# A chunked delta-rule scan rebuilt from 64x64 quarter products, in a four-layer kernel on one core

## The reference

```python
def step(state, inp):                      # state: 64x64 for each head
    r_t, w_t, k_t, v_t, kk_t, b_t = inp
    sa = jnp.einsum('bhij,bhj->bhi', state, kk_t)
    state = (state * w_t[:, :, None, :] - sa[..., None] * b_t[:, :, None, :]
             + v_t[..., None] * k_t[:, :, None, :])
    y_t = jnp.einsum('bhij,bhj->bhi', state, r_t)
    return state, y_t
_, y = lax.scan(step, s0, (seq_first(rh), seq_first(wh), seq_first(kh),
                           seq_first(vh), seq_first(kk), seq_first(bh)))
...
y = group_norm(y) * ln_w + ln_b + bonus    # then * silu(gate), @ w_out
```

## Time and profile before

| | us |
|---|---|
| median of 3 runs | 1167.2 (1166.43 to 1167.28) |
| the profiled execution | 1165.14 |
| its span, first to last instruction | 1162.9 |
| the scan: first product of chunk 0 to the first product of the embedding behind it | 249.8 to 327.3 |
| PE busy over the span | 1130.6 (97%) |
| DVE, ACT, POOL busy | 735.5, 609.0, 465.5 |

### The profile page before, as it was taken

How to read it: one execution, slowest core, us unless ns; L and a number is a source line. 1 busy time by engine, 2 the same in 40 slices (tenths; PEclk the granted TensorE clock), 3 DMA queues, 4 the chain that set the end, 5 groups by cost and what they waited for, 6 DMA issues and landing times.

```text
span 1162.9 us, 19410 instructions
## 1 busy us (share of the span) xinstructions
PE 1130.6 (97%) x7558; PEld 885.5 (76%) x7558; DVE 735.5 (63%) x1166; ACT 609.0 (52%) x1026; POOL 465.5 (40%) x375
## 2 busy tenths in 40 slices
PE   7999999989999999999999999999999999999998
PEld 5756767878867887777777778878888888867776
DVE  6769996966675466666666484473593234567773
ACT  6867445536754466566655554462211344566563
POOL 2331024557733543333332344444454445532240
PEclk9999999999999999999999999999999999999999
DMA  9912446343183633212222123533333333322111
GB/s 285 273 55 73 89 112 217 109 138 80 46 296 97 193 94 90 74 56 73 69 59 73 55 91 93 164 89 88 97 102 91 101 98 91 91 73 67 62 55 73
DMA packets 194684, 123.02 MB, mean 106 GB/s; under 512 B 27877, under 2 KB 181030, under 8 KB 194214
## 3 DMA queue, kind: packets, MB, share of 16 engines
q1 hardware_dynamic: 191990, 119.27, 34.9%
q10 hardware_dynamic: 2608, 2.56, 0.7%
HBM read 105.03 MB, written 16.78 MB: 105 GB/s over the span
## 4 chain that ended last, share of the span: by engine, by line
PE 39%; issue 24%; POOL 12%; DVE 10%; DMA 1%; ACT 1%; POOLq 0%; ACTq 0%; DVEq 0%; SPq 0%
POOL b_w_lo L672 12%; PE banks L760 9%; PE banks L762 9%; PE banks L761 9%; DVE b_problems L2388 2%; DVE b_sum_squares L2386 2%; PE banks L1413 1%; PE banks L1441 1%; DVE b_suffix L2871 1%; PE banks L1020 1%; DMA b_problems<-d_a 1%; PE banks L767 1%; DVE b_a_lo L2217 1%; PE banks L1423 1%; DVE b_h_t L2213 1%
## 5 line engine op out<-in xcount | busy, mean ns | idle before, releaser
L672 POOL TENSOR_TENSOR b_w_lo<-b_w_raw,b_w_hi 128x512 fp32r<-128x512 f32 x296 | 399.5, 1371 | 637.8 <-ACT b_w_hi L1518 637.7
L760 PE MATMUL banks<-b_a_lo,b_w_hi 128*128 128x512 f32 x1232 | 496.6, 403 | 7.8 <-POOL b_w_lo L672 3.4
L762 PE MATMUL banks<-b_a_hi,b_w_lo 128*128 128x512 f32 x1232 | 482.1, 391 | 0.0
L761 PE MATMUL banks<-b_a_hi,b_w_hi 128*128 128x512 f32 x1232 | 481.1, 390 | 0.0
L1518 ACT ACTIVATE b_w_hi<-b_w_raw 128x1024 fp32r<-128x1024 f32 x156 | 164.9, 1057 | 255.1 <-PE banks L762 249.0
L760 PEld LDWEIGHTS banks<-b_a_lo,b_w_hi 128*128 128x128 f32 x1232 | 231.9, 188 | 72.0 <-issue 16.7
L762 PEld LDWEIGHTS banks<-b_a_hi,b_w_lo 128*128 128x128 f32 x1232 | 231.7, 188 | 50.2
L761 PEld LDWEIGHTS banks<-b_a_hi,b_w_hi 128*128 128x128 f32 x1232 | 232.2, 188 | 44.2 <-issue 0.5
L1956 ACT ACTIVATE b_exps<-banks,b_stats 128x128 f32<-128x128 f32 (+3 forms) x64 | 33.2, 524 | 58.3 <-DVE b_stats L2655 58.3
L2511 DVE SCALAR_TENSOR_TENSOR b_a_lo<-b_x_t,b_params,b_a_hi 128x512 fp32r<-128x512 f32 x32 | 34.3, 1085 | 23.5 <-ACT b_a_hi L1858 23.5
L2653 DVE TENSOR_TENSOR banks<-banks,b_consts 128x256 f32<-128x256 f32 x32 | 13.8, 433 | 46.3 <-PE banks L1269 45.1
(11 more groups left out here) (358 smaller groups left out, 1568.2 us busy)
## 6 DMA issues: line engine op xcount, KB each, us to landing
b_w_raw<-rw_w_in SPq DMA_DIRECT2D x32, 512.0 KB, 4.3
b_w_raw<-da_w_in SPq DMA_DIRECT2D x32, 512.0 KB, 4.0
b_w_raw<-w_in_a SPq DMA_DIRECT2D x32, 512.0 KB, 4.0
b_w_raw<-pe_w_gate SPq DMA_DIRECT2D x16, 512.0 KB, 4.2
d_ple<-b_ple_out SPq DMA_DIRECT2D x16, 256.0 KB, 4.5
b_w_raw<-rw_w_out SPq DMA_DIRECT2D x8, 512.0 KB, 4.1
b_ple_in<-d_ple SPq DMA_DIRECT2D x2, 2048.0 KB, 10.4
b_w_raw<-da_w_out SPq DMA_DIRECT2D x8, 512.0 KB, 3.9
```

What stands on the lines that cost most here:

```text
L672: m = pool.tensor_tensor(WLO[:, u % 2, ks], WRAW[:, u, ks], WHI[:, u % 2, ks].bitcast(F32), ALU.subtract)
L760: pe.matmul(dst, hi, a_lo[:, k_act, :], start=first, stop=False)
L761: pe.matmul(dst, hi, a_hi[:, k_act, :], start=False, stop=False)
L762: return pe.matmul(dst, lo, a_hi[:, k_act, :], start=False, stop=last)
```

## The change

- The stacked operands are taken apart. `w_of` becomes `w_values` (masked products with v) and `w_state` (K with the state); `s_of` becomes two calls of `s_part`, one for v and one for u; `y_chunk` becomes four calls of `y_part`. All sums are made in PSUM as before.
- Each product now has 64x64 operands. On which side (partitions 0 to 63 or 64 to 127) a head's operand lies alternates by tile (`side_w`, `side_u`), so that neighbours in the order use different quarters.
- `products` no longer makes the NB-K product: KH is multiplied with K and R (128 columns), NB with R alone (64 columns).
- `rows_of` turns by products with a 64x64 identity, 32 of them a chunk, in place of 8 transposes of 128x128.
- POOL's copies (`place_kt`, `place_v`) are gone. `scale_state` is one operation of 128x512 in place of two of 64x512.
- Copies out of PSUM span 128 partitions: keeping w, u, rows and masked products takes fewer and wider operations on ACT and DVE. ACT makes the table of decays that fits the new placing once (`order_decays`).
- PE's order in a chunk is new, and the parts that need v alone (w, s and y) are put where u and the state are waited for. The first embedding product is split and put into the last chunk.

Cut to its core (the placing of buffers, SP's store of the NB-K products and the checks of other waits left out):

```diff
+def side_w(h, j):
+    return h ^ j % 2
+def side_u(h, j):
+    return h ^ j % 2 ^ j // 2 % 2
+STRAIGHT, CROSSED = ([j for j in range(NT) if side_u(0, j) == n] for n in range(2))
...
-        def place_kt(c):
-            for h, hp in enumerate((low, up)):
-                pool.tensor_copy(XA[hp, :, h, :], KRX[hp, 0, :, chunk(c)]).then_inc(sem("kt_placed"), 1)
-        def place_v(dst, n):
-            for h, hp in enumerate((up, low)):
-                pool.tensor_copy(dst(hp, h), VS[hp, n // 2, :, :]).then_inc(sem("v_placed"), 1)
...
-        def rows_of(c, g):
-            turn_four(NKB, [NKP[:, 4 * g + m].rearrange("p n t -> p (n t)") for m in range(4)]).then_inc(sem("rows_mm"), 1)
+        def rows_of(c, kinds):
+            for kind in kinds:
+                for j in range(NT):
+                    for h, hp in enumerate(halves):
+                        m = pe.matmul(RB_[h][halves[side_u(h, j)], four(256 * kind, j // 2)], NKP[hp, j, kind, :], IDENT[hp, hp], ...)
...
-        def w_of(c):
-            for j in range(NT):
-                for h, hp in enumerate((low, up)):
-                    m = pe.matmul(WB[h][hp, tile_cols(j)], XA[:, j, h, :], SVX[c % 2][:, j, h, :], ...)
+        def w_values(c, tiles):
+            for j in tiles:
+                for h in range(2):
+                    at = halves[side_u(h, j)]
+                    m = pe.matmul(WB[h][halves[side_w(h, j)], four(0, j // 2)], XA[at, j // 4, h, j // 2 % 2, :], VS[at, c, j, :], ...)
+        def w_state(c):
+            pe.wait_ge(sem("state_done"), c)
             for j in range(NT):
+                for h, hp in enumerate(halves):
+                    m = pe.matmul(WB[h][halves[side_w(h, j)], four(0, j // 2)], KRX[hp, 0, j, chunk(c)],
+                                  ST[hp, c % 2, side_u(h, j), j // 2, :], ...)
...
-        def s_of(c):
-                    m = pe.matmul(SB[hp, tile_cols(j)], NKR[:, c % 2, j, h, :], UV[:, j, h, :], ...)
+        def s_part(c, kind):
+                    m = pe.matmul(RB_[b][hp, four(0, j // 2)], NKR[halves[b], h, kind, j // 2, :], VS[halves[b], c, j, :] if kind else u_at(h, j), ...)
-        def y_chunk(c):
-                    m = pe.matmul(y_at(h, j), UV[:, j, h, :], XR[:, c % 2, j, h, :], start=False, ...)
+        def y_part(c, tiles, kind):
+                    m = pe.matmul(y_at(h, j), VS[at, c, j, :] if kind else u_at(h, j), XR[at, c % 2, j // 4, h, j // 2 % 2, 1 - kind, :], ...)
...
+        for c in range(NC - 1):
+            pair = (c + 1) // 2 if c % 2 else 0
+            if c:
+                w_state(c)
+                products(c + 1, 0)
+                y_state(c)
+            u_of(c)
+            y_part(c, STRAIGHT, 1)
+            s_part(c, 1)
+            if pair:
+                first_corner(pair)
+            if c:
+                products(c + 1, 1)
+            s_part(c, 0)
+            y_part(c, STRAIGHT, 0).then_inc(sem("y_half"), 1)
...
```

More of the change, by code:

```diff
@@ L827, in ple_out @@
                 low_ready(pe, g + 1)
-            for k in range(2):
+            for k in ks:
                 if n == 0 and layer == 0:
@@ new lines, in products @@
+            for pair in ((0, 1), (3, 2)):
+                for kind, width in ((1, 2), (0, 1)):
+                    for m in pair:
+                        j = 4 * g + m
+                        for h, hp in enumerate(halves):
+                            o = j // 2 % 2 * 256 + (0 if kind else 2 * CH)
+                            last = pe.matmul(xb[h][halves[side_u(h, j)], o:o + width * CH], NKX[hp, kind, j, chunk(c)],
+                                             KRX[hp, 2 - width:, j, chunk(c)], start=True, stop=True, skip_group_check=True)
@@ L1145, in second_embedding, with y_state @@
-        def second_embedding(n):
-            if n == 0:
+        def y_state(c):
+            y_free(c)
+            for j in range(NT):
+                for h, hp in enumerate(halves):
+                    pe.matmul(y_at(h, j), ST[hp, c % 2, side_u(h, j), j // 2, :], KRX[hp, 1, j, chunk(c)], start=(j < 2), stop=False,
+                              skip_group_check=True)
+        def y_part(c, tiles, kind):
+            if kind:
+                pe.wait_ge(sem("x_kept"), 4 * c + 4)
+            else:
+                pe.wait_ge(sem("u_kept"), 2 * c + 2)
+            for j in tiles:
+                for h in range(2):
+                    at = halves[side_u(h, j)]
+                    m = pe.matmul(y_at(h, j), VS[at, c, j, :] if kind else u_at(h, j), XR[at, c % 2, j // 4, h, j // 2 % 2, 1 - kind, :],
+                                  start=(kind == 1 and c == 0 and j in (0, 3)), stop=(kind == 0), skip_group_check=True)
+            return m
@@ L1738, in bonus_out, with order_decays @@
             act.dma_start(D_BV[j], TMP[:, 2 + j % 2, :]).then_inc(sem(f"bv_out{j % 2}"), 16)
+        def order_decays():
+            act.wait_ge(sem("el_done"), NT)
+            for h, hp in enumerate((low, up)):
+                for b in range(2):
+                    for j1 in range(2):
+                        act.activation(PCS[hp, :, b, :, j1], PC[hp, :, 2 * j1 + (h ^ b ^ j1)::4], ACT.Copy)
         def keep_gate(j):
@@ L1810, in keep_y @@
+        def keep_y(c, h):
             act.wait_ge(sem("yx_mm"), c + 1)
[L1811 to L1840 removed]
```

403 lines of the change are left out of this document (197 added, 206 removed).

## The result

| | before | after |
|---|---|---|
| median, us | 1166.8 (1165.9 to 1167.3, 4 runs) | **1196.8** (1195.5 to 1200.9, 4 runs) |
| ratio to before | | 1.026, 95% interval 1.0243 to 1.0282 |
| the profiled execution, us | 1165.1 | 1196.8 |
| its span | 1162.9 | 1195.0 |
| the scan | 249.8 to 327.3 | 249.4 to 359.8 |

The change costs 30 us, where +20 was forecast; 1196.8 lies just over the range's end of 1196. Nearly all of it is in the scan: the centering behind it starts 31.6 us later, and the whole execution is 31.7 us longer.

What follows compares the result with a forecast made beforehand. Instruction supply to PE, 3.6 us per 256, bounds the scan: start to 252.4, then 4.1, 90.0 and 1.0 end it at 347.5, +20.2; centering -0.8, queueing +0.6; net +20, median 1187, range 1181 to 1196.

Steps and rivals of the forecast that it cites:

- What bounds the kernel: PE's instructions come in blocks of 256, one block ahead; a round of fetching takes 3.6 us whatever PE could do.
- the edge at 252.4: Scan's start: first block boundary, 138 instructions behind the scan's first product, reached from 249.8 to 252.4.
- the first stop's end at 256.5: Scan's start: first round of instruction supply, with transfers dense, forecast at 4.1 us.
- "issue": PE idle time in the scan that the profile calls issue: some 25 stops of 1.2 to 1.6 us, 30 us in all.
- The first rival: Scan: supply isn't the limit and blocks come as PE needs them; about -10 us, 1157; chance 0.07.
- the half-way one: Scan: a supply round of 2.8 us, time within 0.2% of before; chance 0.04.
- ACT, DVE and POOL cost nothing: Scan: PE's waits for these engines fall into the instruction-fetch stops, costed at nothing.
- The length of a round: Scan: after the first round, 25 rounds of 3.6 us for 256 PE instructions each, 90.0 us.
- The bound of 3.9: Scan: upper bound on a round, 3.9 us with queueing, giving +9 us on the forecast time.
- Queueing: Instruction packets queued behind block loads for a round or two: +0.6 us.
- the third rival: Scan: granted clock falls, a block takes 4.0 us: +10, and 3 behind the scan, 1200; chance 0.03, shared with waits between blocks.
- The end of the scan: Last part of a block with half of the first embedding product: 1.0 us, scan ending at 347.5.

Runs made afterwards that it cites:

- experiment 1: Kernel before with 64x64 products of 256, 64 and 16 columns added behind its last awaited instruction, needing no data: 64-column rounds 3.61 us on the mean.
- The probes: Two kernels: before plus data-free 64x64 products behind its end, without loads (3.61 us a round) or with 2 MB loads (3.76 us a round; 1269.3 us whole).
- Experiments 5 and 6: Kernel after, 1 MB and 2 MB loads both cut (1202.2) or only the second (1193.4); before plus 1792 products, 2 MB loaded whole, then in pieces: 1269.3 us.
- experiment 3: Kernel after without y's masked products for three of four tiles from chunk 1 on, 336 pairs fewer: 1185.7 us, ratio 1.0155 to before.
- experiment 4: Kernel after with all products of NB and KH 128 columns wide, same instruction count: 1197.6 us, ratio 1.0272; after beside it 1199.4, ratio 1.0274.
- experiment 5: Kernel after, loads behind the state: both in four parts, 1202.2 us; first whole, second in four, 1193.4; the latter with 128-column products, 1195.6.
- before_halves: Kernel before with each product of w, u, s and y cut into two of 32 columns, 992 pairs more: 1200.6 us, ratio 1.029.

## Why the prediction was right or wrong

**What bounds the kernel: right.** The blocks of 256, the one block ahead, the edge at 252.4 (found at 251.7) and the first stop's end at 256.5 (256.4) all came as worked out, and the packets are 27 against about 27. That "issue" is 30.1 us against 30 forecast is luck in part: 6.2 of it is the one stop behind the loads, and there are 20 stops and not 25, because PE at half clock was still at work when some blocks came. The first rival (blocks come as PE needs them, 1157) is gone by experiment 1, the half-way one too: no round was 2.8 us. That ACT, DVE and POOL cost nothing held: 2.9 us in the four largest of their waits, most of it inside a round.

**The length of a round: the first term that failed.** The mechanism was right; what failed is the size of terms of the sum. It had 25 rounds of 3.6, from two pairs of packets 3.7 and 3.4 apart. They were 3.84 on the mean over the 23 rounds from 256.4 to 344.7, 88.2 us where the sum had 82.8: **+5.4 us**. The forecast took the middle of what the kernel before showed; but that kernel often reached an edge late, so that its spacing was partly PE's and partly the supply's. The probes, with nothing but the supply, have 3.61 and 3.76; the thirteen rounds of after at the full clock have 3.86, made of 1.30 until the packet starts, 1.16 for the packet and 1.41 until PE goes on. The bound of 3.9 was drawn for this, with +9, and the rounds alone stayed within it.

**Queueing: mis-sized by its largest case.** The sum had +0.6 for packets behind block loads. One packet stood behind 3 MB, and its round took 8.46: **+4.9 over 3.6**. The rows for it were at hand: SP's two loads are there before too, and that kernel's instruction queue is silent from 319.2 to 327.9 in the same place. It cost nothing there, because PE had 128-row pairs and then embedding products of 230 ns each to go through, and a block of those lasts far longer (the round from 331.35, with the centering in it, took 32.6 us). The prediction read the last part of the scan as if only PE's work lay there. Experiments 5 and 6 show the mechanism, and with experiment 3 its price: 3 MB issued 1.1 to 1.5 us ahead of an edge add 4.9 us to a round, issued just behind the edge 1.5; 2 MB add 3.0 to 3.2, pieces of 0.5 MB nothing.

**The clock: the third rival was partly true.** The prediction held stops of 1.5 us to be too short for the clock to fall. It fell six times. The lower level is the 0.50 or 0.51 of the granted clock: in the kernel before, at 0.51, seven products of 512 columns started 0.427 us apart from 18.31 to 21.30, 1.20 columns a ns, which is what the 1.2 GHz of the prediction amounts to; at 1.00 such products started 0.226 us apart from 328.01 to 329.82. By stretch, PE working and stopping, the half clock behind it, and the same ahead of 327.7, where it fell again:

```profile
267.95:273.05 5.10, 2.31 (x128) 2.16 (x127) 1.45 (x3) 2.61 (x7) 1.90 (x1) 1.00 0.81 159
273.10:276.50 3.40, 3.40 (x118) 3.28 (x119) 0.42 (x1) 0.38 (x1) 0.00 (x0) 0.50 0.02 5
...
323.20:327.70 4.50, 2.06 (x125) 1.92 (x121) 1.59 (x4) 1.01 (x3) 1.29 (x1) 1.00 0.21 63
```

After 5.1 us with 2.3 of work, one of its stops 2.3 long, the clock is at 0.50. In these stretches PE works a block off in 3.6 to 4.4 us and has hardly a stop left, so that the half clock mostly fills the stops. The rival's +10 didn't come: no price of the clock in the middle of the scan is told apart from the spread of the rounds, and by experiment 4 it is at most 1 to 3 us.

**The end of the scan: the third term.** The scan's end is 6.7 us behind the edge at 353.1 where 4.6 were forecast, **+2.1**. The clock has some 0.9 of this: the block ran at half clock until 358.4, and in the execution of experiment 5 at full clock the same work took 5.8 us (354.5 to 360.3). The other 1.2 are the forecast's: one more round of over 3.6, and a last part with the embedding's first half of about 1.6 us where the sum had 1.0.

Together: +5.4 +4.9 +2.1 = 12.4, for 12.3 between the forecast end of the scan, 347.5, and the measured 359.8. Behind it the centering starts 1.9 us later, forecast 2.0. The 0.6 that the sum had for queueing comes off: 11.7 between the forecast +20.0 and the profiled execution's +31.7. By the medians it is 9.8, since the profiled execution of before lay 2.1 us under its median and that of after on it. The mechanism was right and the size was too small in three terms, all on the same side; the range held each of them alone, and not the three together.

**What stays open**: why packets in some stretches are asked for 0.3 to 0.8 us later than in others with no load near, when exactly the clock falls, since two executions of the same kernel differ in it, and what it costs.

## What to carry to other kernels

Count PE's instructions as well as its work: here 256 of them, 128 pairs, took 3.6 to 3.9 us on the mean wherever PE stood waiting for them, so a pair costs at least 28 to 30 ns, and splitting a product into cheaper ones pays only while the mean pair stays above that. Two 64x64 products at 16 ns each in place of one of 34 ns gain nothing on PE and double the supply. In a stretch that lives on the supply, look at what transfers of 1 MB or more are queued when an edge is crossed (the round was 5.2 us behind 1 MB, 6.8 behind 2 MB, 8.5 behind 3 MB); cut them, but not the one that PE reads next.

## What the runs showed of the hardware

- A pair in two quarters of the array costs 31 ns with 32 columns (before_halves) and 34 ns with 64 (before); alternating over four quarters it costs 15 to 16 ns with 64 columns (after, before), 27 with 128 (before) and 54 with 256 (probe).
- Rounds of the supply come in steps: 3.47, 3.75 and 4.02 us from stop to stop in both probes, with no load near.
- A packet of instructions isn't served ahead of data: behind 2 MB it started 4.3 us after its edge, behind 3 MB 6.0, behind pieces of 0.5 MB 1.1. Nor does it wait for the load's end: the last transfers of those loads started 3.2 and 5.1 us after it.
- The granted clock fell from 1.00 to 0.50 while PE worked in bursts of 2.1 to 2.3 us with stops of 1.4 to 2.4 between them, in the kernel and in the probe (0.50 from 1225 to 1235), and in after once 4.7 us into the stop of 6.2; two executions of one kernel had it at different places (0.50 from 273.1 to 276.5 in after's first, from 275.4 to 282.2 in its second).
